# Latent attention in a two-block model: values as the stationary operand for a pair of heads, row sums from ScalarE, inverses spread by TensorE

## The reference, cut to what matters

```python
def causal_block_attention(q, k, v, scale):          # q, k: (1, 512, 6, 96); v: (1, 512, 6, 64)
    def one_block(args):                             # blk: 128 query tokens, all keys
        s = jnp.einsum('bhqd,bkhd->bhqk', q_blk, k).astype(jnp.float32) * scale
        s = jnp.where(k_pos[None, :] <= q_pos[:, None], s, -jnp.inf)
        p = jax.nn.softmax(s, axis=-1).astype(v.dtype)
        return jnp.einsum('bhqk,bkhd->bqhd', p, v)

mix = jnp.concatenate([y_a, y_b, y_c], axis=-1)      # y_c: the attention, 384 of 1024 channels
x = x + mix @ w_out[l]
```

## Time and profile before

| | |
|---|---|
| time, median of 3 runs | 3386.72 us (3386.57 to 3386.79) |
| the profiled execution | 3385.45 us, its span 3383.7 us |
| PE, DVE, ACT, POOL busy | 99%, 49%, 31%, 46% of the span |
| instructions of the span | 43406 |
| the attention loop, first layer of the second block | 2371.5 to 2408.0 us |
| the same in the second layer | 2943.2 to 2979.8 us |

### The profile page before, as it was taken

The page is one execution under the profiler, slowest core; times in us unless marked ns, Lnnn a source line. Parts: engine busy times, 40 slices in busy tenths (PEclk is TensorE's granted clock), DMA queues, the critical chain, the costliest instruction groups (busy, mean ns, idle before and its releaser), DMA issues.

```text
span 3383.7 us, 43406 instructions
## 1 busy us (share of the span) xinstructions
PE 3366.7 (99%) x15386; PEld 2735.5 (81%) x15386; DVE 1662.8 (49%) x2047; ACT 1051.6 (31%) x1412; POOL 1547.2 (46%) x1160
## 2 busy tenths in 40 slices
PE   9999999999999999999999999999999999999999
PEld 7888877788888888887778888887888888788887
DVE  5442236754423644223575442378680727867161
ACT  3222234332222322223443222236421123642122
POOL 4444443354544544444335444453354543435443
PEclk9999999999999999999999999999999999999999
DMA  4333322233332333333223333242232333223332
GB/s 152 99 95 97 110 77 69 75 100 99 93 105 88 101 98 93 99 110 84 63 81 89 102 96 106 84 106 61 64 99 97 96 99 77 63 73 106 94 99 81
DMA packets 496294, 311.32 MB, mean 92 GB/s; under 512 B 41804, under 2 KB 454963, under 8 KB 496179
## 3 DMA queue, kind: packets, MB, share of 16 engines
q1 hardware_dynamic: 494316, 307.21, 31.0%
q10 hardware_dynamic: 1863, 2.51, 0.2%
HBM read 306.01 MB, written 3.67 MB: 92 GB/s over the span
## 4 chain that ended last, share of the span: by engine, by line
PE 64%; issue 19%; POOL 13%; DVE 3%; DVEq 1%; ACT 0%; POOLq 0%; DMA 0%; ACTq 0%
POOL wl L501 13%; PE bank L545 11%; PE bank L549 11%; PE bank L551 9%; PE bank L526 9%; PE bank L531 9%; PE bank L530 9%; PE bank L552 1%; PE mb L608 1%; DVE small L2380 0%; DVE sd_p L2302 0%; PE mb L1179 0%; PE bank L1154 0%; PE mb L1101 0%; DVEq L2089 0%
## 5 line engine op out<-in xcount | busy, mean ns | idle before, releaser
L501 POOL TENSOR_TENSOR wl<-raw,wh 128x512 fp32r<-128x512 f32 x1152 | 1546.1, 1363 | 1802.1 <-ACT wh L1331 1801.8
L1331 ACT ACTIVATE wh<-raw 128x1024 fp32r<-128x1024 f32 x576 | 608.6, 1057 | 1621.8 <-PE bank L526 824.6
L545 PE MATMUL bank<-xh,wh 128*128 128x512 f32 x2384 | 933.5, 392 | 0.0
L549 PE MATMUL bank<-xl,wh 128*128 128x512 f32 x2384 | 927.7, 389 | 0.0
L551 PE MATMUL bank<-xh,wl 128*128 128x512 f32 x2086 | 811.9, 389 | 0.0
L545 PEld LDWEIGHTS bank<-xh,wh 128*128 128x128 f32 x2384 | 447.5, 188 | 102.9 <-issue 10.2
L549 PEld LDWEIGHTS bank<-xl,wh 128*128 128x128 f32 x2384 | 447.7, 188 | 92.5 <-issue 1.0
L526 PE MATMUL bank<-hh,wh 128*128 128x512 f32 (+1 forms) x1216 | 472.5, 389 | 0.0
L530 PE MATMUL bank<-hl,wh 128*128 128x512 f32 (+1 forms) x1216 | 472.2, 388 | 0.0
L531 PE MATMUL bank<-hh,wl 128*128 128x512 f32 (+1 forms) x1216 | 472.2, 388 | 0.0
L551 PEld LDWEIGHTS bank<-xh,wl 128*128 128x128 f32 x2086 | 391.6, 188 | 82.0
(11 more groups left out here) (418 smaller groups left out, 3169.5 us busy)
## 6 DMA issues: line engine op xcount, KB each, us to landing
raw<-in_ffn_wi_dram SPq DMA_DIRECT2D x176, 512.0 KB, 3.7
raw<-in_mlp_w_dram SPq DMA_DIRECT2D x128, 512.0 KB, 3.7
raw<-in_w_in_dram SPq DMA_DIRECT2D x102, 512.0 KB, 3.6
raw<-in_ffn_wo_dram SPq DMA_DIRECT2D x88, 512.0 KB, 3.6
raw<-in_w_out_dram SPq DMA_DIRECT2D x32, 512.0 KB, 3.8
raw<-in_w_ple_gate_dram SPq DMA_DIRECT2D x16, 512.0 KB, 3.8
raw<-in_w_a_dram SPq DMA_DIRECT2D x8, 512.0 KB, 3.3
raw<-in_w_b_dram SPq DMA_DIRECT2D x8, 512.0 KB, 3.3
```

The costliest lines, as they stand in the source:

```text
L501: last = gp.tensor_tensor(wl[j][:, part], raw[j % RAW_SLOTS][:, part], wh[j][:, part].bitcast(F32), ALU.subtract)
L545: first = pe.matmul(out[0:width, :], h[:, c:c + width], rh[:, k, :], start=k == 0, stop=False)
L549: pe.matmul(out[0:width, :], h[:, c:c + width], rl[:, k, :], start=False, stop=False)
L1331: act.activation(wh[n % SPLIT_SLOTS][:], raw[n % RAW_SLOTS][:], ACT.Copy).then_inc(s.hi_ready, 1)
```

## The change

`weighted` no longer works block by block. It is called for a pair of heads, at c = 9, 17 and behind the loop. `v_tok` of a head (128 x 64) is now the stationary operand and `prob_t` the moving one. The two heads of a pair write partitions 0 to 63 and 64 to 127 of one PSUM bank, so the result has channels on partitions, and `pair_turned`, `o_tok` and `head_scaled` go. `prob_t` becomes three whole heads. The sums come from ACT's `Exp` (`accum_out`) into `row_sum`, 24 columns of `small`. DVE inverts eight of them at a time (`shares`), PE spreads them over 64 partitions per head by a matmul against the identity (`share_rows`), DVE copies that to `tmp[1]`, multiplies the pair by it and splits the product. The two splits of the other branch move from c = 8 and 16 to before the loop. The logits' distance stays at three.

```diff
-        o_tok = at_kb("o_tok", 46, [P, NT, 384])
-        prob_t = at_kb("prob_t", 52, [P, 4, S])
+        prob_t = [at_kb(f"prob_t{h}", kb, [P, NT, S]) for h, kb in enumerate((24, 52, 44))]
+        row_sum = small[:, 4:28]
...  TensorE
+                def weighted(i):
+                    pe.wait_ge(s.at_copied, at(L, 24, 8 * i + 8))
+                    if i:
+                        pe.wait_ge(s.ao_done, at(L, 3, i))
+                    for j in range(NT):
+                        for side in range(2):
+                            h = 2 * i + side
+                            last = pe.matmul(mb[64 * side:64 * side + 64, 2 + i % 2, j * P:S], v_tok[:, j, h, 0:64],
+                                             prob_t[h % 3][:, j:NT, j * P:(j + 1) * P], start=j == 0, stop=j == NT - 1)
+                    last.then_inc(s.ot_ready, 1)
+                def share_rows(i):
+                    pe.wait_ge(s.as_ready, at(L, 3, i + 1))
+                    if i:
+                        pe.wait_ge(s.ao_done, at(L, 3, i))
+                    else:
                         pe.wait_ge(s.y_read, at(L, 1, 1))
+                    for n in range(NT):
+                        for side in range(2):
+                            c = (2 * i + side) * NT + n
+                            last = pe.matmul(mb[64 * side:64 * side + 64, 3 - i % 2, n * P:(n + 1) * P],
+                                             row_sum[:, c:c + 1].to_broadcast([P, 64]), ident, start=True, stop=True)
+                    last.then_inc(s.ir_ready, 1)
                 for c in range(blocks):
...
                     turned(c)
-                    if c:
-                        weighted(c - 1)
-                    if c in (11, 19):
-                        pair_turned(c // 8 - 1)
-                weighted(blocks - 1)
+                    if c in (9, 17):
+                        share_rows(c // 8 - 1)
+                        weighted(c // 8 - 1)
+                share_rows(2)
+                weighted(2)
...
-                        elif u == 0:
-                            pair_turned(2)
...  ScalarE
-                act.activation(v_tok[:, :, :, 64], ones[:, 0:NT * MLA_H].rearrange("p (t h) -> p t h", t=NT), ACT.Copy)
...
+                    if c in (12, 20):
+                        act.wait_ge(s.ot_ready, at(L, 3, c // 8))
+                    act.activation(prob_t[c // NT % 3][:, n, 0:(n + 1) * P], mb[:, c % 2, 0:(n + 1) * P], ACT.Copy)\
                        .then_inc(s.at_copied, 1)
...
-                                   bias=small[:, 32 + n:33 + n], scale=-1.0).then_inc(s.ae_ready, 1)
+                                   bias=small[:, 32 + n:33 + n], scale=-1.0, accum_out=row_sum[:, c:c + 1]).then_inc(s.ae_ready, 1)
...  VectorE
                 dve.drain().then_inc(s.rot_done, 1)
+                for k in range(2):
+                    split(xh[:, k, :], xl[:, k, :], proj2[:, k, :]).then_inc(s.ssd_done, 1)
...
+                def shares(i):
+                    dve.wait_ge(s.ae_ready, at(L, 24, 8 * i + 8))
+                    dve.reciprocal(row_sum[:, 8 * i:8 * i + 8], row_sum[:, 8 * i:8 * i + 8]).then_inc(s.as_ready, 1)
+                def share_rows(i):
+                    dve.wait_ge(s.ir_ready, at(L, 3, i + 1))
+                    dve.tensor_copy(tmp[1][:], mb[:, 3 - i % 2, :])
                 def pair_split(i):
                     dve.wait_ge(s.ot_ready, at(L, 3, i + 1))
-                    split(xh[:, 5 + i, :], xl[:, 5 + i, :], mb[:, 3, :]).then_inc(s.ao_done, 1)
+                    dve.drain()
+                    dve.tensor_tensor(tmp[2][:], mb[:, 2 + i % 2, :], tmp[1][:], ALU.mult)
+                    dve.drain()
+                    split(xh[:, 5 + i, :], xl[:, 5 + i, :], tmp[2][:]).then_inc(s.ao_done, 1)
...
                     if c in (8, 16):
-                        k = c // 8 - 1
-                        split(xh[:, k, :], xl[:, k, :], proj2[:, k, :]).then_inc(s.ssd_done, 1)
-                    if c >= NT and c % NT == 1:
-                        head_scaled(c // NT - 1)
+                        shares(c // 8 - 1)
+                    if c in (10, 18):
+                        share_rows(c // 8 - 1)
                     if c in (12, 20):
                         pair_split(c // 8 - 1)
-                head_scaled(MLA_H - 1)
+                shares(2)
+                share_rows(2)
                 pair_split(2)
+                dve.drain()
```

More of the change, by code:

```diff
@@ L51 @@
 MLA_D = 96
+LOOK = 3
 DT_COL = 1536
@@ L288, in program @@
             c_squared c_ss c_read c_inv c_rs c_ready small_landed gv_added rk_psum rot_done
-            key_rows al_ready am_ready ae_ready at_ready at_copied ao_ready ao_scaled ot_ready ao_done
+            key_rows al_ready am_ready ae_ready at_ready at_copied as_ready ir_ready ot_ready ao_done
             fin_squared gained fin_turned fin_copied fin_scaled stored""".split()
@@ L1166, in turned @@
                     last.then_inc(s.at_ready, 1)
[L1168 to L1172, removed]
-                        pe.wait_ge(s.y_read, at(L, 1, 1))
[L1174 to L1188, removed]
+                def weighted(i):
[8 more added lines that the diff above has]
+                    last.then_inc(s.ot_ready, 1)
@@ L1190, in mla @@
                 blocks = NT * MLA_H
-                for c in range(3):
+                for c in range(LOOK):
                     logits(c)
                 for c in range(blocks):
-                    if c + 3 < blocks:
-                        logits(c + 3)
+                    if c + LOOK < blocks:
+                        logits(c + LOOK)
                     turned(c)
-                    if c:
-                        weighted(c - 1)
-                    if c in (11, 19):
-                        pair_turned(c // 8 - 1)
@@ L1663, in copied @@
                     act.wait_ge(s.at_ready, at(L, 24, c + 1))
-                    act.activation(prob_t[:, c % 4, 0:(n + 1) * P], mb[:, c % 2, 0:(n + 1) * P], ACT.Copy)\
+                    if c in (12, 20):
+                        act.wait_ge(s.ot_ready, at(L, 3, c // 8))
+                    act.activation(prob_t[c // NT % 3][:, n, 0:(n + 1) * P], mb[:, c % 2, 0:(n + 1) * P], ACT.Copy)\
                        .then_inc(s.at_copied, 1)
@@ L2393, in scan_split @@
                        .then_inc(s.ssd_done, 1)
[L2395 to L2401, removed]
-                                      share[:, :, None].to_broadcast([P, NT, 64]), ALU.mult).then_inc(s.ao_scaled, 1)
+                def shares(i):
[4 more added lines that the diff above has]
+                    dve.tensor_copy(tmp[1][:], mb[:, 3 - i % 2, :])
                 def pair_split(i):
                     dve.wait_ge(s.ot_ready, at(L, 3, i + 1))
-                    split(xh[:, 5 + i, :], xl[:, 5 + i, :], mb[:, 3, :]).then_inc(s.ao_done, 1)
+                    dve.drain()
+                    dve.tensor_tensor(tmp[2][:], mb[:, 2 + i % 2, :], tmp[1][:], ALU.mult)
+                    dve.drain()
+                    split(xh[:, 5 + i, :], xl[:, 5 + i, :], tmp[2][:]).then_inc(s.ao_done, 1)
                 blocks = NT * MLA_H
```

## The result

The changed kernel takes 3396.01 us, the median of eight runs (3394.29 to 3397.34). The kernel before, run beside it, takes 3385.97 (eight runs, 3385.39 to 3386.79). The ratio is 1.003, with a 95% interval of 1.0022 to 1.0039: 10.0 us or 0.30% slower, inside the predicted range of 3385 to 3398, and 4.0 above the predicted 3392.0. The forecast of a difference was 5.6 us, so that is 4.4 short; 3392 stood on the 3386.72 of the first three runs of before, 0.75 above the median of all eight.

What follows compares the result with a forecast made beforehand. TensorE was followed as the bound, DVE pacing the loop's first half; the summed steps put the projection 3.2 us later, less 0.4 for the turned pair: +2.8 per layer, +5.6 for both, hence 3392 us, range 3385 to 3398.

Steps and rivals of the forecast that it cites:

- Up to the first spread: First layer, DVE-bound start of the loop until PE first spreads the inverses: that point at 2384.8 us.
- First to second spread: First layer, PE's piece at c = 9 to that at c = 17, with `pair_split` at 2.75: 12.7 us.
- Second to third spread: PE's piece at c = 17 to the one behind the loop, `pair_split` 1.9 beside idle POOL: 10.3 us.
- The third piece: Last pair's spread and weighted sum, now wholly ahead of the projection: 3.4 us, ending at 2411.2.
- The waits: PE idle about 1.2 us before block 15's transposes and 2 us before block 23's, put down to the exponential.
- Weighted 2.3, spread 1.0, entry 0.1: PE's cost per pair: weighted matmuls 2.3 us, spreading inverses 1.0, entering the half-width form 0.1; 3.4 in one piece.
- Spread one half at a time: Rival: inverses' halves run singly on PE, 1.8 us not 1.0, 3397.1; chance 0.17 shared with both splits slow.
- Sums by ACT: Accumulator reads after ACT's exponentials: no throughput cost, but the result comes 0.1 us later on the path.
- Tile 2 needs `scan_split`, slack 0.1: Projection's output tile 2: `scan_split` done 11.6 us after projection start, PE there at 11.7, so nothing added.
- PE never waits: Rival: DVE and ACT keep up behind PE's pieces, -2.3 us per layer, 3382.1; chance 0.17.
- It hides: Rival: projection or weight stream has unseen slack and the end does not move, 3386.7; chance 0.08.
- The clock falls: Rival: PE's clock drops to 1.2 GHz after idling before the last transposes, +6.8 us, 3399; chance 0.05.

## Why the prediction came out as it did

I had called anything within 0.2% the same, and my 3392 stood at 0.16%. The result is 0.30%, slower: the less likely way (0.35 for slower, 0.60 for the same). The waits and the three pieces came as forecast, and the range held; but 3.5 of the 10.0 us come from the clock, which my forecast put at nothing and left to a rival of 0.05. By the steps of the sum:

- *Up to the first spread*, predicted 13.1 us after the first logits (2384.8 less 2371.67): 13.09 and 13.08.
- *First to second spread*, predicted 12.7: 14.17 in the first layer, 12.86 in the second. This is a mis-sized term, the new `pair_split`. I took 2.75, from a cast of 0.42 and a subtraction of 1.60. The second layer had 2.79. In the first VectorE stood idle for 0.44 us ahead of the product, which the trace puts down to no one (`issue`); so POOL began 0.08 us ahead of the cast, where it was 0.20 behind it in the second, and the cast took 1.47. That makes 3.82, and 1.5 us more than the 12.7. I had priced the cast from the split that stood beside an idle POOL, and looked at the slow subtraction alone in the other; its cast, just ahead of the row shown in the earlier trace rows, took 0.93 in that trace.
- *Second to third spread*, predicted 10.3: 10.29 in both layers.
- *The third piece*, predicted 3.4: 3.18 in the second layer, 4.86 in the first, for the clock.
- *The projection 39.5 us after the first logits*: 39.41 in the second layer, 42.41 in the first.
- *The waits*, predicted 1.2 and 2 us: 2.70 and 1.97 in the first layer, 1.39 and 1.97 in the second, put down to the exponential as said. I named only these two; the others (0.90 before block 13, 0.41 before the first spread, and more) make up the rest of the 8.7 and 7.4.
- *Weighted 2.3, spread 1.0, entry 0.1*: 2.26, 0.92, and about 0.15 (2398.87 to 2399.24 is 0.37 for two transposes of 0.11). *Spread one half at a time* falls.
- *Sums by ACT*, 0.1 late on the path: 0.26 us per layer at a steady clock in the run that has them alone.
- *The moved splits hidden*: shown, and alone the move is 3.6 us. I had counted it in the sum, in the start of the first spread, and never priced it by itself.
- *Tile 2 needs `scan_split`, slack 0.1*: its end came 11.6 us after the projection's start again, with no wait of PE. Right.

**The rivals.** *PE never waits* fell: the waits came. *It hides* fell: the end moved with the projection's start. *PE never waits* has a slip of 0.1 us in its sum, too small to matter: blocks 10 to 23 are 37 transposes, 4.1 us at 0.11 and not 4.2. *The clock falls*, given 0.05, is the part that I had too low. I priced it as the whole last piece twice as long, 3.4 us in every layer, and found the wait near the 1.58 us that did no harm before. What happened lies between: a fall that cost 1.7 us in the changed kernel's trace and 1.3 to 3.0 in those of the other runs, behind either wait, in some layers of some runs, some 3.5 us in the median. And 1.58 was no safe length: with ScalarE's sums in the old kernel one run fell behind 1.67.

So the 10.0 us are, from the runs: 6.5 at a steady clock (3392.51 less 3385.97), and 3.5 for the clock. By the traces the 6.5 are the predicted 5.6, and 1.3 for the pause of 0.44 and the slow cast of the first layer alone (14.17 less 12.86), less 0.2. As the fall comes behind the waits, and the two longest waits come from one place in VectorE's list, 7.0 of the 10.0 went with the move of one call. What remains in the 3389.0 are the other waits, 6.3 us per layer against 1.6 before, from which the 2.7 us of saved work are to be taken: ScalarE's rounding ahead of block 13 is one of them. I have not taken them apart one by one.

One thing I had wrong in the explanation and not in the sum: that TensorE's piece starves VectorE of block 13's logits, "and everything restarts from there". At block 13 ScalarE's rounding was the later one. What the late logits of block 14 cost by themselves no run here isolates.

## What to carry to other kernels

When work spread thinly over a loop is gathered into one piece, look at the lists of the other engines: what they do with the piece's result must stand behind what the gathering engine needs next, and moving one such call by one place was worth 7 us of 10 here. Time a change that bundles an unrelated gain (the moved splits, 3.6 us) by its parts, and give that gain to the old form too before comparing. A wait of 2 us on TensorE can cost more than itself here: filling it with nothing useful gave 2.8 us back, filling it with work that had to be done anyway 6.9.

## What the runs showed of the hardware that I had not expected

- The same wait of 1.97 us before the same transposes was followed by a fall of the clock to 1.2 GHz in the first layer and not in the second layer of one run. Over the runs of one kernel the times then form steps: about 3389.3, 3391.5 and 3394.2 us with the rounding moved.
- Nor was a wait of that length needed. With ScalarE's sums in the old kernel the clock fell behind a wait of 1.67 us. With the piece behind the next logits the waits ahead of the last piece were 0.39 and 0.68 us in the profiled run, and the third spread and weighted sum were recorded with 1.76 and 3.40 us, at a mean clock of 0.66 in the 5 us from 2406. With the split's place alone the same two waits, 0.40 and 0.68, left them at 1.09 and 2.32.
- A cast from float32 with one SBUF input, 0.43 us alone, took 1.47 when it began 0.08 us behind a subtraction of POOL, and 0.43 when it began 0.20 us ahead of one. A subtraction of two SBUF tensors went from 0.69 to 1.60.
- Two products with 64 stationary columns each, written to the two halves of a PSUM bank, ran side by side in float32 for 128 moving columns as for 512: eight products of 128 columns (sixteen instructions) in 0.92 us.
